# Attention's value products in 32-column pieces, and the decode loop written out, in a hybrid SSD and latent-attention layer

## What is computed

```
def block_causal_attention(q, k, v):          # 8 heads, q and k of width 96, v of width 64
    ...
        s = jnp.einsum('bqhd,bkhd->bhqk', qb, kp).astype(jnp.float32) * ATTN_SCALE
        ...
        p = jax.nn.softmax(s, axis=-1)
        return jnp.einsum('bhqk,bkhd->bqhd', p.astype(vp.dtype), vp)

def paged_attention(q, k_new, v_new, lat_pool, kr_pool, layer, page_table, w_ukv, gk):
    ...
    def page_step(carry, pids):               # 32 pages of 128 positions for each of 8 samples
        k, v = mla_keys_values(lat_pool[layer, pids], kr_pool[layer, pids], w_ukv, gk)
        return update(carry, k, v, None), None
```

## Time and profile before

| | |
|---|---|
| median of 3 runs | 2168.37 us (2168.35 to 2169.13) |
| the profiled execution | 2171.12 us, its span 2169.2 us |
| PE busy in the span | 2000.2 us (92%) |
| PE weight loads | 1608.6 us |
| DVE, ACT, POOL busy | 1197.6, 630.0, 633.8 us |
| mean granted TensorE clock | 0.965 of full speed |
| attention's matmuls begin and end | about 474 to 647 us |
| decode's slots | 677 to 1213 us |

### The profile page before, as it was taken

The page is one execution under the profiler, slowest core; times in us unless marked ns, Lnnn a source line. Parts: engine busy times, 40 slices in busy tenths (PEclk is TensorE's granted clock), DMA queues, the critical chain, the costliest instruction groups (busy, mean ns, idle before and its releaser), DMA issues. The chain is left out here.

```text
span 2169.2 us, 35266 instructions
## 1 busy us (share of the span) xinstructions
PE 2000.2 (92%) x12575; PEld 1608.6 (74%) x12575; DVE 1197.6 (55%) x2030; ACT 630.0 (29%) x1319; POOL 633.8 (29%) x586
## 2 busy tenths in 40 slices
PE   8999999759988999898999569799999999999998
PEld 4566676436657777776777448699989999998997
DVE  4577667747744865665666435354444444444444
ACT  2232323224434444443444222121111111111110
POOL 1343443420005433232333133243222322323211
PEclk9999999869998999999999889899999999999999
DMA  5011111156311012232223140212220122102201
GB/s 218 21 37 37 41 37 51 35 120 145 105 43 33 21 51 66 63 89 66 57 69 79 42 165 29 58 40 59 59 59 26 34 59 59 40 20 60 59 20 78
DMA packets 180740, 132.77 MB, mean 61 GB/s; under 512 B 61757, under 2 KB 165486, under 8 KB 180438
## 3 DMA queue, kind: packets, MB, share of 16 engines
q1 hardware_dynamic: 177190, 129.37, 20.8%
q0 software_dynamic: 144, 1.08, 0.2%
q10 hardware_dynamic: 3232, 0.01, 0.1%
HBM read 110.81 MB, written 19.65 MB: 60 GB/s over the span
## 5 line engine op out<-in xcount | busy, mean ns | idle before, releaser
L2460 PE MATMUL f_ps<-nT_hi,f_gu_hi 128*128 128x344 f32 x1056 | 338.9, 321 | 11.0 <-POOL f_gu_lo L2332 6.7
L2460 PE MATMUL f_ps<-nT_hi,f_gu_lo 128*128 128x344 f32 x1056 | 337.9, 320 | 1.1 <-issue 1.1
L2460 PE MATMUL f_ps<-nT_lo,f_gu_hi 128*128 128x344 f32 x1056 | 337.6, 320 | 0.0
L1568 POOL TENSOR_TENSOR s_b_latT<-s_b_latT_hi,s_b_latT_lo 128x1024 f32<-128x1024 f32 x64 | 153.5, 2398 | 354.7 <-DVE s_b_latT_lo L1622 354.6
L1689 DVE TENSOR_REDUCE s_b_ssq<-s_b_ksq 128x8 f32<-128x512 f32 x256 | 172.9, 685 | 120.3 <-ACT s_b_ksq L1487 118.2
L1487 ACT ACTIVATE s_b_ksq<-s_ps 128x512 f32<-128x512 f32 x256 | 153.6, 600 | 216.6 <-PE s_ps L1840 173.1
L1840 PE MATMUL s_ps<-s_b_wk_hi,s_b_latT_hi 128*128 128x512 f32 x512 | 208.4, 407 | 7.0 <-ACT s_b_ksq L1487 7.0
L2460 PEld LDWEIGHTS f_ps<-nT_hi,f_gu_hi 128*128 128x128 f32 x1056 | 199.4, 189 | 14.7 <-issue 7.1
L1840 PE MATMUL s_ps<-s_b_wk_hi,s_b_latT_lo 128*128 128x512 f32 x512 | 202.1, 395 | 0.0
L1840 PE MATMUL s_ps<-s_b_wk_lo,s_b_latT_hi 128*128 128x512 f32 x512 | 202.0, 395 | 0.0
L2460 PEld LDWEIGHTS f_ps<-nT_lo,f_gu_hi 128*128 128x128 f32 x1056 | 198.8, 188 | 0.4
(11 more groups left out here) (370 smaller groups left out, 3592.2 us busy)
## 6 DMA issues: line engine op xcount, KB each, us to landing
p_latn<-in_cache_kv_latent SPq DMA_DIRECT2D x256, 128.0 KB, 2.0
gu_raw<-in_w_gate SPq DMA_DIRECT2D x22, 512.0 KB, 4.1
gu_raw<-in_w_up SPq DMA_DIRECT2D x22, 512.0 KB, 5.3
f_wd_raw<-in_w_down SPq DMA_DIRECT2D x11, 1024.0 KB, 5.1
t_w_in<-in_w_in SPq DMA_DIRECT2D x8, 980.0 KB, 13.0
t_x<-in_x_prompt SPq DMA_DIRECT2D x8, 512.0 KB, 5.6
p_krn<-in_cache_k_rope SPq DMA_DIRECT2D x256, 16.0 KB, 1.8
h<-in_w_out SPq DMA_DIRECT2D x8, 512.0 KB, 8.5
```

The lines of the kernel that those rows point to most:

```text
L1568: out(pool.tensor_tensor(out=flat(latT), in0=flat(latT_hi).bitcast(F32), in1=flat(latT_lo).bitcast(F32), op=ALU.add), "sum_done")
L2460: ins = pe.matmul(ps[:, bank + j, 0:W], w[fi][:, j, k, :], x[:, k, cols], start=(k == 0 and w is gu_hi and x is nT_hi), stop=(k == KD - 1 ...
```

## The change

Three things are edited. In `values` each 64-column product becomes two 32-column products, so four of them stand side by side over the 128 PSUM partitions for a pair of heads. The decode loops of TensorE, VectorE, ScalarE, GpSimd and SyncE become Python loops, so that samples 1 to 6 (2 to 7 on SyncE) are written out, with constants in place of registers, and VectorE's step counter needs no loop bookkeeping. The page registers are named by sample.

```diff
@@ Pages.load
-            with sp.register(f"page{'_first' if isinstance(b, int) else ''}{p}_{pg}") as reg:
+            with sp.register(f"page{b}_{pg}") as reg:
@@ attention_block, values
-                        ins = pe.matmul(ps[i * VD:(i + 1) * VD, O_BANK, w * P:(w + 1) * P], v[:, b, h * VD:(h + 1) * VD],
-                                        pt[g][pt_slot(n)][:, c, :], start=(b == 0), stop=(b == t))
+                        for lo in range(0, VD, QT):
+                            ins = pe.matmul(ps[i * VD + lo:i * VD + lo + QT, O_BANK, w * P:(w + 1) * P],
+                                            v[:, b, h * VD + lo:h * VD + lo + QT], pt[g][pt_slot(n)][:, c, :],
+                                            start=(b == 0), stop=(b == t))
@@ samples_block, SyncE
-        with sp.Fori(1, NS // 2) as i:
+        for i in range(1, NS // 2):
@@ samples_block, ScalarE (GpSimd and TensorE alike)
-        with act.Fori(0, 3) as i:
+        for i in range(3):
@@ samples_block, VectorE
-        with dve.Fori(0, 3) as i:
-            dve_steps.begin(i, 14)
+        for i in range(3):
...
-            dve_steps.end(3)
```

More of the change, by code:

```diff
@@ L1597, in _ @@
         pool.dma_start(a["ssm_sample"][0].rearrange("b h p n -> (b h) p n"), h0[:, :, :]).then_inc(y_stored, 16)
-        with pool.Fori(0, 3) as i:
+        for i in range(3):
             for p, b in ((1, i * 2 + 1), (0, i * 2 + 2)):
@@ L1875, in _ @@
             slot(0, 0, g, True, False)
-        with pe.Fori(0, 3) as i:
+        for i in range(3):
             for p, b in ((1, i * 2 + 1), (0, i * 2 + 2)):
```

## The result

The changed kernel takes 2141.32 us (2140.74 to 2146.14, 4 runs) where the kernel before takes 2168.75 (2168.35 to 2171.56, 4 runs): a ratio of 0.9876, 95% interval 0.9859 to 0.9893. The profiled execution of after takes 2141.36 us, its span 2139.8, which is 29.4 less than that of before; the kernel before was profiled 2.4 us above its median, so the pair of profiles overstates the gain by about 2 us.

What follows compares the result with a forecast made beforehand. TensorE's stream, busy 2000.2 of 2169.2 us, was taken as the bound. Loop -15.9, pages -0.6 and products -1.0 sum to -17.5 us: 2153.6 for a profiled execution, 2150.9 for the median, range 2146 to 2159.

Steps and rivals of the forecast that it cites:

- The loop written out, -15.9: Decode: removing two taken branches brings two slots to 7.51 us, saving 8.15 and 7.73 us, together 15.9; lower bound 10.8.
- the register work on each engine runs beside the matmuls and I cost it at nothing: Decode loop: TensorE's products cover the register work, since slots inside a pass (7.50) and outside (7.51) are equally long.
- Nothing is to be won at the loop's entry or exit: Decode: entering or leaving the loop costs nothing, read from one slot of 7.51 us where the loop is left.
- the slot at 1147.50: Decode: slot from the loop's last pass into written-out code, 7.51 us, taken as the measure of a plain slot.
- no slot without a branch gap shows the slow clock: Decode: the 1.2 GHz stretch comes behind the branch gap only, the reason for taking 15.9 us and not 10.8.
- Pages, -0.6: Decode, SyncE's page loads: one register instruction less per page issues groups 0.2 us sooner at three samples; between -2.8 and +2.8.
- Products, -1.0: Attention's value products: 1152 records of 32 columns, four side by side, replace 576; between -3.2 and +0.6 us.
- since TensorE has no idle time in this stage: Attention: no work is hidden beneath the value products, so a microsecond there is a microsecond at the end.
- Rival A: Attention: the four product pieces don't overlap four deep, so the kernel is slower, +15.1 us, 2183; 4 in 100.
- it is the taken branch of a long loop that is dear: Decode: TensorE's taken branches took 3917 and 3517 ns, against 218 to 238 ns in the mixing stage's short loop.
- Rival B: Decode: instruction fetching as such stalls, so written-out code stalls as often and decode gains nothing, 2167 us; 5 in 100.
- Rival C: Decode: samples 3 and 5 give back some 4 us each to hidden waits, mainly pages; sum -9.5, 2158.9 us; 12 in 100.

Runs made afterwards that it cites:

- sp_loop: The changed kernel with SyncE's decode loop kept as a hardware loop; 2141.37 us, ratio 0.987.
- decode_only: The changed kernel with the value products on 64 columns as before, so only decode's loops are written out; 2141.41 us, ratio 0.9873.

## Why the prediction was right, and where it was wrong

**The loop written out, -15.9: right for the profiled pair.** The two slots measure 7.51 us, and 15.67 + 15.25 - 2 x 7.51 = 15.9. That this is also the kernel's usual gain isn't shown: the surplus of the two slots was 9.6 to 17.3 us over the four kernels with all loops, 14.3 in the mean. And the sentence that it is TensorE's taken branch that is dear was half of it. With TensorE's loop alone written out 7.6 of the 15.9 us stay, from ScalarE's stall of 4.6 us and, behind that, VectorE's of 3.4. The stalls lay one beside the other, which is why the slots alone gave the right sum: that was luck as far as the cause goes. That "the register work on each engine runs beside the matmuls and I cost it at nothing" was wrong for what goes with it: each engine's own stall behind its branch.

**"Nothing is to be won at the loop's entry or exit": wrong.** I had looked only at the slot at 1147.50. At the entry, sample 1's second slot lost 3.6 us, because VectorE met GpSimd while it was late from its sum of 4.40 us, and because that made it a slot with a granted clock of 0.87 (the prediction says that no slot without a branch gap shows the slow clock, which is wrong here); between the exit and the mixing stage 1.9 us went. Of that, VectorE's loop had some 0.6 (27.6 to 27.0), and the rest is left with GpSimd's, since sp_loop, which keeps SyncE's, has 25.6 us; no run keeps GpSimd's alone. In the kernel before VectorE waits 2.8 us there for two small transfers, and 1.7 in the changed one.

**Pages, -0.6: too small.** The profiled pair has -3.0. Over all the kernels the last slots' surplus is 1.7 to 3.7 us where TensorE has its branches and 0.7 to 1.9 where it hasn't, so some 1.4 belongs to the change and the rest is scatter. SyncE's loop, from which I had derived the term, has no part in it.

**Products, -1.0: inside its bounds, its size not shown.** The pace is 26.1 ns a record where 27.4 keeps the time, which makes (26.1 - 27.4) x 1152 = -1.5 us. Attention took 171.3 us in the mean of seven kernels with 64 columns (170.6 to 172.1) and 169.8 in seven with 32 (168.5 to 171.1): -1.5 too, but the two groups overlap, and the 2.6 us inside the second come from kernels whose attention code is the same. The medians of decode_only and the changed kernel, 2141.41 and 2141.32 us, show 0.1. That a microsecond here is a microsecond at the end, "since TensorE has no idle time in this stage", was also too strong: from 489 to 648 us it was busy 151.13 of 159 us. Rival A is out: four pieces do run side by side.

**The FFN, absent: this is the step that failed.** The sum has terms for decode's loop, for the page loads and for the products, and it puts everything behind decode at nothing without a reason. From the earlier trace rows the prediction compares decode's branches of 3.5 to 3.9 us with the mixing loop's 0.22 and concludes that "it is the taken branch of a long loop that is dear". The FFN's loop is the other long one, and its branch record, which the prediction doesn't read, was 3.6 us as well. In the changed kernel it is 0.21 us, and the FFN takes 760.8 us in place of 767.9: these 7.1 us are the largest part of the miss. Even with that row in hand its fate would have needed the place of the loop's first instruction in its packet, which a change upstream moves.

Rival B (fetching as such stalls) is out, as code that is written out has no gap; but what it named is the cause behind the branch. Rival C (half given back by the pages) went the other way. The account for the medians: -15.9 - 3.6 - 1.9 - 7.1 - 1.5 for products - 1.4 for pages is -31.4, against 27.4 measured. With the mean of the branch slots (14.3 for 15.9) and the products as the medians have them (0.1 for 1.5) it is -28.4, which is near but proves neither. Decode's plain slots repeat within 0.1 us from kernel to kernel and the FFN within 0.6 in either of its two kinds, but where the tiles end scatters from 459.5 to 463.1 us, so a single profile hardly tells what stands against them.

What stays open besides: why VectorE loses the meeting at sample 1 whenever its own loop is kept, and wins when it is written out; whether TensorE keeps any loop longer than this one, since decode's of 9 packets was dear each time; how many instructions ScalarE, VectorE and GpSimd keep, and why the last's branch was never seen to cost. Shifting decode's loop was not tried.

## What to carry to other kernels

A long hardware loop can have a price per taken branch on several of the engines that run it (here on TensorE, ScalarE and VectorE), and it hides where the profile names no releaser: read the branch records of all loops in the program and the "issue" gaps of all engines behind them, and write out the loops of all engines together or expect to find the next one's stall. A loop that is not changed can still gain or lose when code ahead of it grows; compare its branch record and the instruction queue's packets before crediting an edit with a gain, and a few idle instructions at a place where the engine waits are enough to shift it. And a wait of one microsecond that comes once per sample, like TensorE's behind VectorE's for the last scores, adds up: moving one step gave 7.4 us.

## What the hardware showed that was not expected

- TensorE kept a loop of about 1,610 instructions, 6.3 packets of 16 KB, over five passes with no packet fetched and branches of 0.21 us, or fetched 9 packets in each pass with branches of 3.3 to 3.8 us, by where the loop began in a packet: kept where it touched seven packets (11 kernels), fetched where it touched eight (3 kernels). 70 instructions of padding switched it.
- The length of a branch record tells TensorE's stall (3.6 us) but not the others': ScalarE's is 45 ns with 4.6 us of "issue" behind it, VectorE's 63 ns with 3.4.
- VectorE's 128x256 operation took 0.41 us alone and 2.60 to 2.65 beside GpSimd's of 2.3 to 2.4 us, begun within 30 ns of each other.
- Four 32-column fp32 products side by side give 26.1 ns a record, two of 64 columns 54.8 ns a record, each read from one row of 32.
